# Thirteen norm tiles behind the second LRU pass, and an earlier gating of four mixed halves in blocks 6 and 7

## The reference

```
mod = silu(c) @ w_ada + b_ada          # 6 x 1024 shifts, scales, gates
h   = RMSNorm(x) * (1 + scale1) + shift1
p   = h @ w_in                         # input of four mixers
o_b = mixer_b(p)                       # RG-LRU, stick-breaking attention, gated DeltaNet, RWKV-7
mixed = sum_b sigmoid(h @ w_gate_b + b_gate_b) * (o_b @ w_branch_b)
x  += gate1 * (mixed @ w_out)
h   = RMSNorm(x) * (1 + scale2) + shift2
x  += gate2 * ((gelu(conv(h @ w_gate)) * (h @ w_up)) @ w_down)
out = RMSNorm(x)
```

## Time and profile before

| what | value |
| --- | --- |
| median of three runs | 1966.34 us (1964.09 to 1970.8) |
| the profiled execution's own time | 1966.72 us |
| its span in the profile | 1964.8 us |
| mean granted TensorE clock | 0.985 |
| PE busy | 1881.5 us (96%) |
| DVE busy | 945.9 us (48%) |
| POOL busy | 915.3 us (47%) |
| ACT busy | 472.4 us (24%) |

### The profile page before, as it was taken

The page is one execution under the profiler, slowest core; times in us unless marked ns, Lnnn a source line. Parts: engine busy times, 40 slices in busy tenths (PEclk is TensorE's granted clock), DMA queues, the critical chain, the costliest instruction groups (busy, mean ns, idle before and its releaser), DMA issues.

```text
span 1964.8 us, 33381 instructions
## 1 busy us (share of the span) xinstructions
PE 1881.5 (96%) x14012; PEld 1503.3 (77%) x14012; DVE 945.9 (48%) x1467; ACT 472.4 (24%) x734; POOL 915.3 (47%) x1100
## 2 busy tenths in 40 slices
PE   3999999999999999999999998999999999999995
PEld 1777777767787787787777786788888888888884
DVE  5883478754546546545434824532232323322325
ACT  4351344352212212212213314310110101101103
POOL 2676556523323223223224573464665655655645
PEclk7999999999999999999999999999999999999998
DMA  8561212232122122122125520111111111111112
GB/s 331 179 237 51 86 56 69 81 126 79 59 72 77 60 72 77 61 71 80 42 98 193 207 94 33 33 43 54 53 43 45 52 53 43 49 47 53 43 43 85
DMA packets 69686, 163.48 MB, mean 83 GB/s; under 512 B 5952, under 2 KB 30528, under 8 KB 69568
## 3 DMA queue, kind: packets, MB, share of 16 engines
q1 hardware_dynamic: 62080, 142.88, 21.6%
q10 hardware_dynamic: 7488, 18.88, 2.6%
HBM read 133.16 MB, written 28.57 MB: 82 GB/s over the span
## 4 chain that ended last, share of the span: by engine, by line
PE 45%; POOL 22%; issue 20%; DVE 8%; DMA 2%; ACT 2%; SPq 1%; POOLq 0%; ACTq 0%; DVEq 0%
PE gbank L585 30%; POOL w_hi L507 11%; POOL w_lo L511 10%; PE mbank L903 3%; DMA fa<-in_w_ada 2%; PE gbank L1050 1%; DVE state L2063 1%; DVE fa L1821 1%; PE gbank L903 1%; PE mbank L659 1%; PE mbank L826 1%; PE gbank L680 1%; DVE fa L1749 1%; PE mbank L1064 1%; DVE fa L2127 1%
## 5 line engine op out<-in xcount | busy, mean ns | idle before, releaser
L507 POOL TENSOR_TENSOR w_hi<-w_raw,zero 128x256 fp32r<-128x256 f32 (+1 forms) x520 | 397.6, 795 | 966.5 <-PE gbank L585 796.3
L585 PE MATMUL gbank<-h_hi,w_hi 128*128 128x512 f32 x1680 | 671.4, 400 | 5.4 <-ACT fa L1233 2.7
L585 PE MATMUL gbank<-h_lo,w_hi 128*128 128x512 f32 x1680 | 662.2, 394 | 0.0
L585 PE MATMUL gbank<-h_hi,w_lo 128*128 128x512 f32 x1680 | 660.3, 393 | 0.0
L511 POOL TENSOR_TENSOR w_lo<-w_raw,w_hi 128x256 fp32r<-128x256 f32 (+1 forms) x520 | 464.0, 923 | 10.2
L585 PEld LDWEIGHTS gbank<-h_hi,w_hi 128*128 128x128 f32 x1680 | 316.0, 188 | 84.6 <-issue 14.1
L585 PEld LDWEIGHTS gbank<-h_hi,w_lo 128*128 128x128 f32 x1680 | 315.7, 188 | 68.9 <-issue 2.0
L585 PEld LDWEIGHTS gbank<-h_lo,w_hi 128*128 128x128 f32 x1680 | 316.1, 188 | 67.0 <-issue 3.3
L1141 PE MATMUL mbank<-ra,w_hi 128*128 128x512 f32 x640 | 197.0, 389 | 0.0
L1141 PEld LDWEIGHTS mbank<-ra,w_hi 128*128 128x128 f32 x640 | 120.1, 188 | 25.0
L2221 DVE SCALAR_TENSOR_TENSOR fa<-mbank,mod,fa 128x1024 f32<-128x1024 f32 x40 | 51.4, 1284 | 169.2 <-PE mbank L1141 169.2
(11 more groups left out here) (339 smaller groups left out, 2169.1 us busy)
## 6 DMA issues: line engine op xcount, KB each, us to landing
w_raw<-in_w_tail SPq DMA_DIRECT2D x74, 512.0 KB, 3.5
fa<-in_w_ada SPq DMA_DIRECT2D x48, 512.0 KB, 6.3
w_raw<-in_w_in SPq DMA_DIRECT2D x26, 512.0 KB, 4.0
p_scr<-fa ACTq DMA_DIRECT2D x20, 512.0 KB, 2.6
w_raw<-in_w_mix SPq DMA_DIRECT2D x16, 640.0 KB, 4.0
fa<-in_xT SPq DMA_DIRECT2D x16, 512.0 KB, 7.7
w_raw<-in_w_gate SPq DMA_DIRECT2D x16, 512.0 KB, 3.9
sig_scr<-fa ACTq DMA_DIRECT2D x32, 256.0 KB, 2.0
```

What stands on the lines that cost most here:

```text
L507: last = pool.tensor_tensor(hi[:, c], raw[:, c], zero[:, 0:1].to_broadcast([P, w]), ALU.add)
L585: mm = pe.matmul(gb[bank], w, r, start=(q == 0), stop=(q == 3 * ks - 1))
```

## The change

Tiles 35 to 47 of `w_ada` get the slots 15, 12, 13, 14, ... (`12 + t % 4`), which the LRU passes use. The first four loads wait for the end of the second pass, and the thirteen stand behind units 11, 12 and 13 in SP's order; the group of units 5 to 7 loses one tile in all, and units 8 to 10 have no group any more. DVE reduces all thirteen behind the second pass. As tile 11 is overwritten before that, ACT copies the vector to tile 3 behind its copy of unit 9, and the first attention sigmoid waits for all 48 tiles. ACT's copy of unit 8 waits for 35 tiles only.

In blocks 6 and 7 the table of fills changes, so that the 114th matmul comes in the last level of the inversion; ACT does the fourth sigmoid and a table load ahead of `uw`; DVE gates the third half in level 3 and the fourth where it had gated the third. In blocks 1, 3 and 5 four numbers of the last part of the table change. In the table the groups of numbers are the fills of the scores, of the inversion levels, of the stretch ahead of r3 and of the state stage and norms.

```
-ADA_SLOT = (8, 16, 18, 19)
+ADA_EARLY = 35
+ADA_SLOT = [(8, 16, 18, 19)[_t % 4] if _t < ADA_EARLY else 12 + _t % 4 for _t in range(48)]
+ADA_BEHIND = {4: (20, 24), 5: (24, 28), 6: (28, 32), 7: (32, ADA_EARLY), 11: (ADA_EARLY, 39), 12: (39, 43), 13: (43, 48)}
...
-        True: ((12, 26, 42, 50, 58), (72, 86, 100, 113, 123), 130, (138, 144, 154, 162, 172, 182, 192)),
+        True: ((12, 26, 42, 50, 58), (72, 86, 100, 113, 123), 130, (138, 144, 153, 160, 173, 183, 192)),
...
-        "full": ((10, 22, 38, 43, 50), (64, 78, 92, 104, 113), 121, (130, 138, 150, 164, 180, 198, 216))}
+        "full": ((10, 22, 38, 43, 50), (64, 78, 92, 106, 116), 122, (130, 140, 152, 168, 184, 200, 216))}
...
# SP
-                if t >= 20:
+                if ADA_EARLY <= t < ADA_EARLY + 4:
+                    sp.wait_ge(sem("lru_lo"), 2)
+                elif t >= 20:
                     sp.wait_ge(sem("ada_used"), t - 3)
-                for t in range(4 * u + 4, min(4 * u + 8, 48)):
+                for t in range(*ADA_BEHIND.get(u, (0, 0))):
                     ada_in(t)
...
# ACT
                 if u == 8:
-                    act.wait_ge(sem("ada_used"), 48)
+                    act.wait_ge(sem("ada_used"), ADA_EARLY)
...
+            act.activation(fa[:, 3, :], fa[:, 11, :], ACT.Copy).then_inc(sem("c_moved"), 1)
+            act.wait_ge(sem("c_moved"), 1)
...
                 if p == 0 and part == 0:
                     act.wait_ge(sem("lru_lo"), 2)
+                    act.wait_ge(sem("ada_used"), 48)
...
-                for job in range(3):
+                for job in range(4 if FULL[i] else 3):
                     gate_sig(job)
+                if FULL[i]:
+                    act.preload_act_table_set("natural_log_exp_and_others")
                 act.wait_ge(sem("r3"), at("r3", i))
...
-                gate_sig(3)
-                act.preload_act_table_set("natural_log_exp_and_others")
+                if not FULL[i]:
+                    gate_sig(3)
+                    act.preload_act_table_set("natural_log_exp_and_others")
...
# DVE: every ada_tiles(...) of the pass now stands under "if c == 0:"
-            dve.wait_ge(sem("ada_used"), 48)
+            ada_tiles(ADA_EARLY, 48)
...
+                    if lv == 3:
+                        if i == 0:
+                            gated(1)
+                        elif FULL[i]:
+                            gated(2)
...
-                gated(2)
+                gated(3 if FULL[i] else 2)
                 new_values(0)
...
                 new_values(1)
-                gated(3)
+                if not FULL[i]:
+                    gated(3)
```

More of the change, by code:

```diff
@@ L80 @@
 assert _q == 4 * NB and U_MIX + len(U_KIND) == U_BR
+FULL = [RAW_PER_BLOCK[_i] == 4 for _i in range(NB)]
 LATE_MIX = [JOBS[_i][0][0] == "raw" for _i in range(NB)]
@@ L83 @@
 FILL = {False: ((10, 22, 36, 41, 48), (58, 68, 78, 88, 96), 104, (114, 120, 130, 140, 156, 174, 192)),
-        True: ((12, 26, 42, 50, 58), (72, 86, 100, 113, 123), 130, (138, 144, 154, 162, 172, 182, 192)),
+        True: ((12, 26, 42, 50, 58), (72, 86, 100, 113, 123), 130, (138, 144, 153, 160, 173, 183, 192)),
         "first": ((120, 134, 150, 158, 166), (180, 194, 208, 222, 236), 248, (258, 264, 274, 284, 300, 318, 336)),
-        "full": ((10, 22, 38, 43, 50), (64, 78, 92, 104, 113), 121, (130, 138, 150, 164, 180, 198, 216))}
-FILL_OF = [FILL["first" if _i == 0 else "full" if RAW_PER_BLOCK[_i] == 4 else LATE_MIX[_i]] for _i in range(NB)]
+        "full": ((10, 22, 38, 43, 50), (64, 78, 92, 106, 116), 122, (130, 140, 152, 168, 184, 200, 216))}
+FILL_OF = [FILL["first" if _i == 0 else "full" if FULL[_i] else LATE_MIX[_i]] for _i in range(NB)]
 E_HALF = float(np.exp(-0.5))
@@ L345, in ada_in @@
             def ada_in(t):
-                if t >= 20:
+                if ADA_EARLY <= t < ADA_EARLY + 4:
+                    sp.wait_ge(sem("lru_lo"), 2)
+                elif t >= 20:
                     sp.wait_ge(sem("ada_used"), t - 3)
-                sp.dma_start(fa[:, ADA_SLOT[t % 4], :], a["w_ada"][t]).then_inc(sem(f"ada_in{t % 4}"), 16)
+                sp.dma_start(fa[:, ADA_SLOT[t], :], a["w_ada"][t]).then_inc(sem(f"ada_in{t % 4}"), 16)
             sp.dma_start(fa[:, 11, :], a["c"].to_broadcast([P, D])).then_inc(sem("c_in"), 16)
@@ L1686, in ada_tiles @@
                     dve.wait_ge(sem(f"ada_in{t % 4}"), 16 * ((t - 16) // 4 + 1))
-                    slot = fa[:, ADA_SLOT[t % 4], :]
-                    dve.tensor_tensor_reduce(slot, slot, fa[:, 11, :], 1.0, 0.0, ALU.mult, ALU.add, mod[:, t:t + 1]).then_inc(sem("ada_used"), 1)
+                    if t == ADA_EARLY:
+                        dve.wait_ge(sem("c_moved"), 1)
+                    slot = fa[:, ADA_SLOT[t], :]
+                    dve.tensor_tensor_reduce(slot, slot, fa[:, 11 if t < ADA_EARLY else 3, :], 1.0, 0.0, ALU.mult, ALU.add, mod[:, t:t + 1]).then_inc(sem("ada_used"), 1)
             def softplus(nth, y, n, out_ap):
@@ L1763, in _ @@
                 x_, u_ = fa[:, c, :], fa[:, 12, :]
-                t0 = 22 + 13 * c
+                t0 = 22
                 dve.wait_ge(sem("gb2_read"), c + 1)
@@ L1780, in _ @@
                 ins.then_inc(sem("lru_u"), 1)
-                ada_tiles(t0, t0 + 6)
+                if c == 0:
+                    ada_tiles(t0, t0 + 6)
                 dve.wait_ge(sem("lru_gates"), 2 * c + 2)
@@ L1784, in _ @@
                 dve.tensor_tensor(fa[:, 14, :], fa[:, 14, :], u_, ALU.mult).then_inc(chain, 1)
-                ada_tiles(t0 + 6, t0 + 8)
+                if c == 0:
+                    ada_tiles(t0 + 6, t0 + 8)
                 dve.wait_ge(sem("lru_a"), 3 * c + 1)
@@ L1788, in _ @@
                 n += 2
-                ada_tiles(t0 + 8, t0 + 9)
+                if c == 0:
+                    ada_tiles(t0 + 8, t0 + 9)
                 dve.wait_ge(sem("lru_a"), 3 * c + 2)
@@ L1793, in _ @@
                 dve.scalar_tensor_tensor(fa[:, 13, :], x_, 1.0, fa[:, 13, :], ALU.add, ALU.mult).then_inc(sem("lru_b2"), 1)
-                ada_tiles(t0 + 9, t0 + 11)
+                if c == 0:
+                    ada_tiles(t0 + 9, t0 + 11)
                 dve.wait_ge(sem("lru_a"), 3 * c + 3)
@@ L1803, in _ @@
                 dve.tensor_tensor(u_, u_, fa[:, 2 + c, :], ALU.mult).then_inc(sem("lru_o"), 1)
-                ada_tiles(t0 + 11, t0 + 13)
+                if c == 0:
+                    ada_tiles(t0 + 11, t0 + 13)
                 dve.wait_ge(sem("lru_hi"), c + 1)
                 dve.tensor_tensor(ra[:, 2 + c, :], u_, ra[:, c, :].bitcast(F32), ALU.subtract).then_inc(sem("lru_lo"), 1)
-            dve.wait_ge(sem("ada_used"), 48)
+            ada_tiles(ADA_EARLY, 48)
             for u in range(10, 12):
@@ L2031, in _ @@
                         dve.tensor_tensor(t64(b_["Y"]), t64(mb[bank][:, 0:256]), over4(f"lv{size}"), ALU.mult).then_inc(done(f"{nm}_Ym", i), 1)
-                    if i == 0 and (lv == 1 or lv == 3):
-                        gated(lv // 2)
-                    if i and lv == 1 + LATE_MIX[i]:
-                        gated(1)
+                    if lv == 1:
+                        if i == 0:
+                            gated(0)
+                        elif not LATE_MIX[i]:
+                            gated(1)
+                    if lv == 2 and i and LATE_MIX[i]:
+                        gated(1)
+                    if lv == 3:
+                        if i == 0:
+                            gated(1)
+                        elif FULL[i]:
+                            gated(2)
                     if lv == 2 and ahead:
```

## The result

The changed kernel takes 1957.01 us (median of six runs, 1955.62 to 1958.2), the kernel before in the same comparison 1966.86. The ratio is 0.9945, 95% interval 0.9934 to 0.9956. The forecast was 1955.7 us. The profiled execution took 1957.07 us with a span of 1955.1, 9.7 less than before.

A forecast was written before the change was run, and what follows sets the result against it. PE, 96% busy, was taken as the bound, so gains came only from its waits and low clock. 3.4 + 3.0 + 1.7 + 2.2 + 1.7 + 0.7 - 1.7 = 11.0 us off 1966.7 gave 1955.7, range 1950.5 to 1964.

The forecast's parts named there:

- Unit 9: PE's 2.7 us wait ahead of unit 9, ended by POOL's split, goes, with 1.7 us of low clock behind it.
- The new wait at unit 12: Moved tiles beside POOL's split of unit 12 make PE wait 1.0 us, bounds 0 to 2.5.
- The gating in blocks 6 and 7: Third half gated in level 3, so PE's 1.48 us wait goes in both blocks: 3.0 us gained.
- The wait ahead of the first branch product: End of block 7: loads move earlier, stores land in time, 3.33 us wait shrinks to about 1.1: 2.2 us gained.
- The fall in block 7: The low clock right behind block 7's gating wait goes: 1.7 us gained.
- The clock behind that wait: The low clock behind the wait ahead of the first branch product recovers: 1.7 us gained.
- Blocks 1, 3 and 5: The point at L1020 stays and one matmul of 0.23 us is saved behind it: 0.7 us in all.
- The fall left out: One of three 1.7 us clock falls taken back from the sum, since a fall needn't be bound to its wait.
- the watch on activity: It runs free of the kernel, so places of falls differ between executions; the sum up to 3 us less good.
- My ground for no fall at unit 12: Low clock behind unit 12's new wait counted at nothing; the two 1.48 us waits brought it once in two.
- the exclusive lock: DVE holds the port shared with POOL: unit 12's split about 15 us, the sum 3 us less good.
- the rivals: Tiles take gain back (0.13); stores stay late (0.12); gating wait only moves (0.07); slower, POOL from unit 11 (0.05).

The follow-up runs named there:

- the second profile of after: The kernel after, unchanged, run once more on the same chip as the last experiment kernel: ratio 0.9945 to the kernel before, 1955.61 us.
- the experiment with the freed copy: The kernel before, with ACT's copy of unit 8 waiting for 45 tiles instead of 48: ratio 0.9996 to the kernel before.

## Why the prediction was right

**Unit 9.** Right in cause and size. The predicted 2.7 + 1.7 us can be read without a fall at unit 6 in the second profile of after. The lines are PE at unit 6 and at the transposes before, and at the transposes in that profile:

```profile
120.15 0.50 PE L585 MATMUL gbank<-h_hi,w_hi 128*128 128x512 f32 x1 [2.71 <-POOL w_lo L511]
172.76 1.97 PE L630 MATMUL mbank<-msk,fa 128*128 128x128 f32 x16 [0.69 <-ACT fa L1233]
...
168.21 0.55 PE L635 MATMUL mbank<-msk,fa 128*128 128x128 f32 x3 [0.69 <-ACT fa L1238]
```

From unit 6 to the transposes it is 168.21 - 120.26 = 47.95 us, before 172.76 - 120.15 = 52.61. That is 4.7 us. In the first profile of after it is only 3.3 (170.61 - 121.26 = 49.35), since the clock fell at unit 6. The expectation that under 1 us would be to spare held: the split ended at 158.28, some 0.8 us ahead of the end of unit 8. The tiles themselves ran later than forecast, from 171.64 to 196.2 instead of 169 to 190, at no cost.

**The new wait at unit 12.** I took 1.0 us, within bounds of 0 and 2.5, and it was 0. I had named the pauses of DVE for its loads and given them too little. Even without the large pause the wait is 0.1.

**The gating in blocks 6 and 7.** Right: 3.0 us, both waits. The fourth sigmoid starts 4.7 us ahead of `uw` (945.28 and 949.97), where I had expected over 3, and ACT then waits 2.70 us for r3.

**The wait ahead of the first branch product.** Right in cause, 2.4 us against 2.2, and the hand-over that stays is 0.94 against 1.1. (The profile puts these 0.94 us down to DVE, whose instruction ended at 1057.51; ACT's read of the last raw half ended at 1057.95, and PE started at 1058.16.) From the wait of 0.24 us in block 4 to the first branch product it is 7.3 us less than before (1058.16 - 808.38 = 249.78 against 1067.50 - 810.38 = 257.12): 3.0 + 2.4, 1.7 for the fall in block 7, and 0.2 that I can't place.

**The fall in block 7.** Here the sum was lucky in its profile. Of the five profiles with the old gating order (before and four experiments), only two show a fall behind that wait of 1.48 us, and only one a fall behind the same wait in block 6. In the three without it, the wait ahead of the first branch product is 3.85, 4.18 and 4.04 us instead of 3.33, and the stretch from block 4 is 256.12, 256.50 and 256.35 us instead of 257.12. PE came earlier to the same late store. So this fall cost 0.6 to 1.0 us by the end of block 7, not the 1.7 of its term, and in most of these executions there was none to win back.

**The clock behind that wait.** Mis-sized. The term was 1.7 us; from the first branch product to the next stage at L1064 (L1069 after) it was 58.77 us before (1126.27 - 1067.50) and 58.04 after (1116.20 - 1058.16), 0.7 less. The lines of that stage, before and after:

```profile
1126.27 0.79 PE L1064 MATMUL mbank<-h_hi,w_hi 128*128 128x512 f32 x1 [2.42 <-DVE h_lo L2120]
...
1116.20 0.50 PE L1069 MATMUL mbank<-h_hi,w_hi 128*128 128x512 f32 x1 [2.42 <-DVE h_lo L2147]
```

DVE paces these products, and PE's higher clock at their start turned partly into waits on DVE (0.39, 1.18 and 1.01 us instead of 0.80 and 0.99).

**Blocks 1, 3 and 5.** Wrong by its whole term of 0.7 us. I had kept the later point of L1020 and saved a matmul behind it. In the profile after, the shorter fills made `from_state(1)` and `to_state(1)` wait as well, and the point itself came later, at a different DVE instruction (L1964 instead of L2063). In block 5 the idle time at L1025 fell by 0.36 us, and 0.37 us came ahead of it.

**The fall left out.** I took one of three falls back for no named place, and one came, at unit 6. That it came in this execution is luck: in the second profile of the same kernel it did not, and that span is 12.1 us below before instead of 9.7. By the Trainium skill ("TensorE: Matmul & The Clock Gate", "Part 1: The HAM clock gate") the watch on activity runs free of the kernel. By that rule, the traces agree: two executions of the same kernel, one wait, clock 0.61 and 1.00.

All twelve profiles together (before, after and ten experiments) show how loosely a fall hangs on its wait:

| wait of PE | us | profiles with it | with a fall behind it |
| --- | --- | --- | --- |
| ahead of unit 6 | 2.71 to 3.00 | 10 | 5 |
| ahead of unit 9 | 1.90 to 2.77 | 5 | 3 |
| gating, block 6 | 1.48 | 5 | 1 |
| gating, block 7 | 1.48 | 5 | 2 |
| first branch product, late store or late ACT | 2.28 to 4.18 | 6 | 6 |
| first branch product, hand-over alone | 0.94 | 6 | 0 |

My ground for no fall at unit 12, that a wait must be long to bring one, had one case in two to rest on; it was not put to the test, since the wait did not come.

**The sum.** It was 1.3 us more than the 9.7 by which the span fell: its terms missed by more than that, and partly made up for one another. Better than predicted were unit 9 with no new wait (4.7 against 3.4), the fall (1.4 against 1.7 given back) and the blocks 6 and 7 with the hand-over (7.3 against 6.9); worse were the blocks 1, 3 and 5 (0.8 too much, 0.1 lost instead of 0.7 gained), the branch products (1.0 too much), a start of unit 6 that was 1.1 us later in this execution (121.26 against 120.15, in a part that the change leaves alone; 120.26 in the second profile), and 0.4 behind the branch products.

The other rule that I weighed, the exclusive lock of the Trainium skill ("SBUF — State Buffer", "SBUF: two separate sides"), would by my estimate have had the split of unit 12 at 15 us beside a busy DVE; no run reached that state for a whole split there, the longest was 10.8. Where DVE left no gap, at unit 9 before, the split took 13.4 us, which is less than 15 too. None of the rivals came.

## What to carry to other kernels

When two engines slow each other, a task that is free in time belongs where the other one has slack, not where its own engine has a gap: the moved tiles cost DVE the same and PE nothing. Check a named releaser against the code and to 0.1 us against the end of each engine that the wait asks for; here it was not the one named, and in another execution it was. Take the falls of the clock from more than one profile before you put them into a sum. And ask of a wait on a store what the transfer engines are doing: an earlier gating shortened a wait far behind it because the loads that it released no longer met the last stores.

## What the runs showed of the hardware

A POOL split of 5.15 us took 13.4 beside a DVE without gaps, 10.0 to 10.8 beside one with short gaps, and a DVE reduction took 1.75 us instead of 1.22. A store of 256 KB from ACT's queue held ACT for 5.9 to 7.9 us when it met 3.5 to 5.5 MB of loads issued before it; the median of such stores in the kernel before is 2.0 us. A wait of about 2.7 us of PE was followed by a fall of the clock in some executions and not in others. At unit 6 a fall cost 1.4 us, at unit 9 it cost 1.6 (from unit 9 to the transposes it is 13.46 us before, and 11.87 in the experiment with the freed copy, where no fall followed); ahead of a late store (block 7) or of a DVE that sets the pace (the branch products) it cost 0.6 to 1.0. A single profile of a kernel can be that much off the next at the same code.
